# First mixer of a three-block kernel: the two gate products of a direction packed by row halves, with both bank waits of the second direction in front of its pair

## The chip, the cores and the metric

The kernel runs on one core of one Trainium2 chip. The metric is the device time of one execution in microseconds. Matrix products run on TensorE (PE in the profile), the other engines are ScalarE (ACT), VectorE (DVE), GpSimd (POOL) and SyncE (SP, which here only issues DMAs). Each has its own stream of instructions and waits on counting semaphores.

## The reference

One block of a gated recurrence with neighbourhood attention, then two layers of another kind, all on x of 512 tokens by 1024 channels in float32. What matters here is the recurrence of the first mixer:

```python
def _rglru_scan(xc, w_gates, b_gates, lam):
    xb = xc.reshape(B_, S, LRU_BLOCKS, LRU_BLOCK)          # 16 blocks of 64 channels
    gates = jnp.einsum('bsni,gnio->gbsno', xb, w_gates).reshape(2, B_, S, W)
    gates = gates + b_gates[:, None, None, :]
    r = jax.nn.sigmoid(gates[0])
    i = jax.nn.sigmoid(gates[1])
    log_a = -LRU_C * r * jax.nn.softplus(-lam)
    a = jnp.exp(log_a)
    bx = jnp.sqrt(-jnp.expm1(2.0 * log_a)) * (i * xc)
    _, h = lax.associative_scan(_lin_combine, (a, bx), axis=1)
    return h
```

It is computed twice, for the tokens forward and backward (two directions, each with its own weights). Each of the 16 blocks has its own 64x64 matrix for the gate r and for the gate i. Beside it stand a centred convolution that gives xc, attention over an 8x16 window with 16 heads of 64, and gating of both by projections.

## The kernel before

Channels lie on the 128 partitions and the 512 tokens along the free axis, so one tile of 128 channels holds two blocks of the recurrence and two heads. The large products (`unit(j)`) split each float32 operand into a high and a low fp32r part and take three products of 128x128 by 512 for each of 8 steps: 24 instructions at L1867 to L1869 for one unit. Before a unit can run, ACT rounds its raw weights to the high part wH (L1855) and DVE subtracts to get the low part wL (L1860).

The first mixer has eight bodies, p = 0 to 7, one for each tile of channels. Body p runs the seven units of the next tile (u = p + 1: xr, gr, q, k, v and two output gates) on PE, and between them the small products of its own tile; p = 1 to 6 are a hardware loop, and p = 7 has no units of its own but the first products of the output projection in their place. The order is written out by hand for each engine, and each `slot(j)` of ACT and DVE stands at the place of `unit(j)`. On PE a body is: unit(0), transposes of the previous tile's last probabilities (L522), **gates of direction 0**, the previous tile's second pair of P times V (L536), unit(1), statistics for q and k (L594), unit(2), **gates of direction 1**, four transposes of v (L601), unit(3), scores (L508), three more transposes of v (L608, after ACT has evacuated the first four), unit(4), and so on with probabilities, scores and P times V up to the next unit(0).

On ACT, after slot(3): Ln and Exp for the norms of q and k (L298, L301, each with a table load), `act_gates` of direction 0, slot(4), `act_gates` of direction 1, two square roots (L309, with a table load), the evacuation of v (L311), then q, slot(5), k, the rest of v (L320) and the exponentials of the probabilities (L235). The Ln stands behind the evacuation of gr (L219), which waits for the end of unit(1). DVE then scales the probabilities, runs the two scans (L383 to L388, with the split of slot(6) between them) and the remaining scores, ACT turns the last ones and begins slot(0) of the next body.

In `pe_gates` (L546) the weights of one gate and direction are a 128x128 matrix with the two 64x64 blocks on its diagonal and zeros elsewhere; each product is in plain float32, which the profile shows as two instructions. Gate r goes to bank 4 and gate i to bank 5, full 128 rows each, and ACT takes each bank with one tanh (sigmoid by tanh) of 128x512 (L249), adding the bias column of `hbg`. Direction 1 reuses the banks: its first product waits for the first tanh of direction 0, its second for the second. The scores after unit(3) use the same banks and wait for the tanh of direction 1. SP loads the gate weights of a tile (L180) after the gates of the previous one.

Of the kernel before, what the change touches and what calls it, by code (L numbers as in the profile page):

```python
# [14 lines left out]
P = 128  # L15
# [25 lines left out]
ACT = mybir.ActivationFunctionType  # L41
# [16 lines left out]
def wait(eng, sem, value):  # L58

    if not (isinstance(value, int) and value <= 0):  # L60
        eng.wait_ge(sem, value)
# [64 lines left out]
def gated_recurrence_mixer(k, st, t, site):  # L126
# [32 lines left out]
    run = scratch("m1", "run", [2, RUN])  # L159
    bias = scratch("m1", "bias", [2, 4, 256])  # L160
    mask = scratch("m1", "mask", [3, 256])
    gate_w = scratch("m1", "gate_w", [4, P])
    mx = scratch("m1", "mx", [8])
    den = scratch("m1", "den", [8])
    M = k.sems("m1_", "evac gab_free zeroed sqk g2 g2p gth gelu qk_stat qk_rs qk_rr qkn conv gates gate_act t2_sqrt lru ix "
# [72 lines left out]
    def act_probT(act, p, s):  # L238
        act.wait_ge(M.p_tr, 4 * p + (s + 1))
        wait(act, M.pv, 4 * p + (s - 1))  # L240
        act.activation(probT[:, s % 2], bank[6][:], ACT.Copy).then_inc(M.p_ev, 1)

    def act_gates(act, p, d):

        for g, dst in ((0, t2), (1, ti)):
            act.wait_ge(M.gates, 4 * p + (2 * d + g + 1))
            wait(act, M.lru, 6 * p + (3 * d - 3))
            n = (2 * d + g) * 8
            act.activation(dst[:, d], bank[4 + g][:], ACT.Tanh, scale=0.5, bias=k.colat(k.hbg, n, p))\  # L249
               .then_inc(M.gate_act, 1)  # L250
        act.wait_ge(M.gate_act, 8 * p + (4 * d + 1))
        act.wait_ge(M.qk_stat, 2 * p + 2)
        sc = k.colat(k.nsp4, 8 * d, p)
        act.activation(la[:, d], t2[:, d], ACT.Exp, scale=sc, bias=sc).then_inc(M.gate_act, 1)
        sc = k.colat(k.sp2, 8 * d, p)
        act.activation(t2[:, d], t2[:, d], ACT.Tanh, scale=sc, bias=sc).then_inc(M.gate_act, 1)

    def act(act, after):
        def body(p, units, prev, tail):
            u = p + 1  # L260

            def slot(j):
                if units and not (isinstance(u, int) and u == 0 and j < st.early):
                    k.split_hi(act, st, u, j)
                if not units and j < after.early:
                    k.split_hi(act, after, 0, j)
            slot(0)
            if tail:
                act_probT(act, p - 1, 2)
            if prev:  # L270
                evac(act, p, 5)
                for n in range(2):
                    wait(act, M.lru, 6 * p)
                    act.wait_ge(M.evac, PER * p + (3 + n))
                    act.activation(sqk[:, n], qk[:, n], ACT.Square).then_inc(M.sqk, 1)
                wait(act, M.y1, 2 * p)
                act.activation(g2[:], gr[:], ACT.Square).then_inc(M.g2, 1)
            slot(1)
            if tail:
                act_probT(act, p - 1, 3)  # L280
            if prev:
                evac(act, p, 6)
                act.wait_ge(M.g2p, 2 * p + 2)
                act.activation(g2[:], g2[:], ACT.Tanh, scale=GELU_C).then_inc(M.gth, 1)
            slot(2)
            if units:
                evac(act, u, 0)
            slot(3)
            if units:
                evac(act, u, 1)  # L290
            if tail:
                act.wait_ge(M.y_f, p)
                act.activation(k.tile_of(k.H, site.y + p - 1), y[:], ACT.Copy).then_inc(M.y_hi, 1)
            if prev:

                for n in range(2):
                    act.wait_ge(M.qk_stat, 2 * p + (n + 1))
                    act.activation(qkr[:, n], bank[6 + n][:], ACT.Ln, bias=k.eps_col[:]).then_inc(M.qk_rs, 1)  # L298
                for n in range(2):
                    act.wait_ge(M.qk_rs, 4 * p + (n + 1))  # L300
                    act.activation(qkr[:, n], qkr[:, n], ACT.Exp, scale=-0.5).then_inc(M.qk_rs, 1)  # L301
                act_gates(act, p, 0)
            slot(4)
            if prev:
                act_gates(act, p, 1)
                wait(act, M.hsum, p)
                for d in range(2):
                    act.wait_ge(M.gate_act, 8 * p + (4 * d + 4))
                    act.activation(sq[:, d], t2[:, d], ACT.Sqrt).then_inc(M.t2_sqrt, 1)  # L309
                act.wait_ge(M.v_tr, 2 * p + 1)  # L310
                act.activation(v_tok[:, 0:4], bank[6][:].rearrange("p (a n) -> p a n", a=4), ACT.Copy)\  # L311
                   .then_inc(M.v_ev, 1)
            if units:
                evac(act, u, 2)
            slot(5)
            if units:
                evac(act, u, 3)
            if prev:
                act.wait_ge(M.v_tr, 2 * p + 2)
                act.activation(v_tok[:, 4:7], bank[6][:, 0:384].rearrange("p (a n) -> p a n", a=3), ACT.Copy)\  # L320
                   .then_inc(M.v_ev, 1)
                act_probs(act, p, 0)
                act_probs(act, p, 1)
            slot(6)
            if units:
                evac(act, u, 4)
            if prev:
                act_probT(act, p, 0)
                act_probs(act, p, 2)
                act_probs(act, p, 3)  # L330
                act_probT(act, p, 1)
# [41 lines left out]
        dve.tensor_tensor(both, both, by, ALU.mult).then_inc(M.scaled, 1)  # L373

    def dve_ix(dve, p, d):
        dve.wait_ge(M.gate_act, 8 * p + (4 * d + 2))
        dve.scalar_tensor_tensor(ti[:, d], ti[:, d], 1.0, xc[:], ALU.add, ALU.mult).then_inc(M.ix, 1)

    def dve_lru(dve, p, d):
# [119 lines left out]
    def pe_score_pair(pe, p, pr):  # L499

        if pr == 0:
            pe.wait_ge(M.qkn, 2 * p + 2)
            pe.wait_ge(M.gate_act, 8 * p + 6)
        else:
            pe.wait_ge(M.biased, 8 * p + 4)
        for b in range(2):
            n = 2 * pr + b
            last = [pe.matmul(bank[4 + hh][:, 256 * b:256 * b + 256],  # L508
                              qkn[64 * hh:64 * hh + 64, 0, P * n:P * n + P],
                              qkn[64 * hh:64 * hh + 64, 1, KSTART[n] * ROWS:KSTART[n] * ROWS + 256],  # L510
                              start=True, stop=True) for hh in range(2)]
        for l in last:
            l.then_inc(M.scores, 1)
# [26 lines left out]
            l.then_inc(M.pv, 1)  # L540

    def pe_gates(pe, p, d):
        for g in range(2):
            if d == 1:
                pe.wait_ge(M.gate_act, 8 * p + (g + 1))
            pe.matmul(bank[4 + g][:], gate_w[:, 2 * d + g], xc[:], start=True, stop=True).then_inc(M.gates, 1)  # L546

    def v_ready(pe):
        return lambda f: pe.wait_ge(S.v_ready, site.v0 + f + 1)
# [2081 lines left out]
def laid_out(x):  # L2631
# [24 lines left out]
    out = shape_constants()  # L2656
    out["cols"] = np.ascontiguousarray(np.concatenate(pieces, 1))
    out["xT"] = np.ascontiguousarray(x["x"][0].T.reshape(DT, P, SEQ).swapaxes(0, 1))
    gates = np.zeros((8, P, 4, P), np.float32)
    g = x["lru_w_gates"][0].reshape(4, 8, 2, 64, 64)  # L2660
    for half in range(2):
        gates[:, 64 * half:64 * half + 64, :, 64 * half:64 * half + 64] = g[:, :, half].transpose(1, 2, 0, 3)
    out["gate_w"] = gates
    rpb = np.zeros((16, RPB_DR, RPB_W), np.float32)
    rpb[:, :, 16:16 + RPB_DC] = x["rel_pos_bias"][0]
# [38 lines left out]
```

## Time and profile before

| what | value |
|---|---|
| median of 3 runs | 2438.6 us (2436.75 to 2439.14) |
| the profiled execution: time, span | 2440.55 us, 2438.4 us |
| PE, DVE, ACT, POOL busy | 97%, 53%, 41%, 7% of the span |
| mean granted clock of PE | 0.986 |
| instructions at L546 | 64, 592 ns median |
| tanh at L249 | 32, some 675 ns each |
| the first mixer in the span | about 414 to 828 us |

The span is the time between the first and the last instruction in the trace, and the execution's time holds 2.15 us more around it. An instruction's duration on PE, ACT or DVE overlaps with that of the next one, so what it costs in a row of instructions is the distance between starts. "64*128 64x512" on a product means weights of 64 rows by 128 columns and a moving operand of 64 rows by 512 columns. In a timeline, brackets hold the idle time before the instruction and what ended it.

### The profile page before, as it was taken

The numbers are of one execution on the slowest core, as the hardware profiler recorded it, in microseconds if no ns is written. First come the engines' busy times: TensorE is split into PE (matmuls) and PEld (weight loads), VectorE is DVE, ScalarE is ACT, GpSimd is POOL, SyncE is SP. The second block draws the span as 40 slices with busy tenths as digits, with TensorE's granted clock in tenths as the row PEclk, the third lists the DMA queues.
The fourth block names the chain that finished last, engine by engine and source line by source line (L and its number), as shares of the span: only waits on it lengthen the run. The fifth ranks groups of instructions, "written<-read, shape, count | busy, mean of one in ns | idle before, by whom it ended". The sixth has DMA issues, their size and how long they took to land.

```text
span 2438.4 us, 30936 instructions
## 1 busy us (share of the span) xinstructions
PE 2360.7 (97%) x10918; PEld 1899.4 (78%) x10918; DVE 1299.3 (53%) x1832; ACT 994.9 (41%) x1481; POOL 176.7 (7%) x140
## 2 busy tenths in 40 slices
PE   8999999999999799999999989999989998999998
PEld 6888887777776588888877768888877766888887
DVE  5443436556666544443365566555248986655524
ACT  4223223676666532222234444333234454433322
POOL 0000002333554000000000000000000000000000
PEclk9999999999999899999999989999999999999999
DMA  4333322222223132233232222223313222232321
GB/s 162 97 100 102 102 90 84 86 88 97 89 73 99 38 101 95 95 111 104 70 102 83 86 69 84 97 96 109 100 47 104 70 70 69 78 103 95 117 95 47
DMA packets 62183, 219.91 MB, mean 90 GB/s; under 512 B 7664, under 2 KB 12272, under 8 KB 62112
## 3 DMA queue, kind: packets, MB, share of 16 engines
q1 hardware_dynamic: 60944, 216.86, 26.9%
q10 hardware_dynamic: 1168, 2.12, 0.3%
q8 instruction: 43, 0.70, 0.1%
q14 instruction: 28, 0.23, 0.0%
HBM read 216.83 MB, written 2.12 MB: 90 GB/s over the span
## 4 chain that ended last, share of the span: by engine, by line
PE 87%; ACT 5%; DVE 4%; issue 4%; ACTq 0%; DMA 0%; DVEq 0%; SPq 0%
PE bank L1867 27%; PE bank L1869 26%; PE bank L1868 26%; ACT m_prob L235 1%; PE bank L546 1%; DVE wL L1860 1%; ACT wH L1855 1%; PE bank L536 1%; PE bank L978 0%; PE bank L1006 0%; PE bank L988 0%; PE bank L1566 0%; PE bank L2239 0%; PE bank L2238 0%; PE bank L2237 0%
## 5 line engine op out<-in xcount | busy, mean ns | idle before, releaser
L1867 PE MATMUL bank<-H,wH 128*128 128x512 f32 x3012 | 1193.2, 396 | 34.9 <-DVE L L1941 15.4
L1869 PE MATMUL bank<-H,wL 128*128 128x512 f32 x3012 | 1176.9, 391 | 0.0
L1868 PE MATMUL bank<-L,wH 128*128 128x512 f32 x3012 | 1176.2, 390 | 0.0
L1860 DVE TENSOR_TENSOR wL<-raw,wH 128x1024 fp32r<-128x1024 f32 (+1 forms) x361 | 475.9, 1325 | 615.5 <-ACT wH L1855 615.5
L1867 PEld LDWEIGHTS bank<-H,wH 128*128 128x128 f32 x3012 | 567.9, 189 | 165.2 <-issue 22.4
L1869 PEld LDWEIGHTS bank<-H,wL 128*128 128x128 f32 x3012 | 567.8, 189 | 120.5
L1868 PEld LDWEIGHTS bank<-L,wH 128*128 128x128 f32 x3012 | 568.4, 189 | 118.7 <-issue 3.8
L1855 ACT ACTIVATE wH<-raw 128x1024 fp32r<-128x1024 f32 (+1 forms) x361 | 396.0, 1105 | 225.4 <-PE bank L1869 204.5
L2059 ACT ACTIVATE H<-prod 128x512 f32 (+1 forms) x88 | 55.7, 632 | 243.5 <-DVE prod L2124 243.5
L2104 DVE TENSOR_TENSOR gate_s<-bank,rstd 128x512 f32<-128x512 f32 x88 | 60.8, 691 | 113.7 <-PE bank L1869 110.7
L641 POOL TENSOR_TENSOR m_bias<-m_run,m_mask 128x256 f32<-128x256 f32 x64 | 75.8, 1221 | 408.1 <-DMA m_run<-in_rpb 408.1
L2124 DVE TENSOR_TENSOR prod<-silu_g,bank 128x512 f32<-128x512 f32 x88 | 60.3, 685 | 79.7 <-PE bank L1869 73.6
L1936 ACT ACTIVATE H<-xT,cols 128x512 fp32r<-128x512 f32 (+1 forms) x56 | 39.9, 723 | 149.5 <-DVE xT L2386 119.0
L2048 ACT ACTIVATE silu_g<-gate_s 128x512 f32<-128x512 f32 x44 | 27.9, 633 | 162.0 <-DVE gate_s L2104 162.0
L2051 ACT ACTIVATE silu_g<-gate_s,cols 128x512 f32<-128x512 f32 x44 | 35.9, 815 | 114.5 <-DVE gate_s L2104 114.5
L2115 DVE SCALAR_TENSOR_TENSOR silu_g<-gate_s,cols,silu_g 128x511 f32<-128x511 f32 x88 | 66.1, 751 | 30.7 <-ACT silu_g L2051 25.1
L2128 DVE TENSOR_TENSOR L<-prod,H 128x512 f32 (+1 forms) x88 | 60.1, 683 | 3.0 <-ACT H L2059 2.8
L2055 ACT ACTIVATE silu_g<-silu_g 128x512 f32<-128x512 f32 x44 | 27.8, 632 | 76.8 <-DVE silu_g L2115 76.8
L235 ACT ACTIVATE m_prob<-m_prob,m_mx 128x256 f32<-128x256 f32 x64 | 32.0, 501 | 66.3 <-DVE m_mx L363 66.2
L1374 DVE SCALAR_TENSOR_TENSOR m_acc<-m_gp,cols,m_acc 128x512 f32<-128x512 f32 x84 | 57.5, 745 | 0.0
L1916 ACT ACTIVATE square<-mixT 128x512 f32<-128x512 f32 (+1 forms) x28 | 17.7, 633 | 94.6 <-DVE mixT L2377 51.2
L1941 DVE SCALAR_TENSOR_TENSOR L<-xT,cols,H 128x512 fp32r<-128x512 f32 (+1 forms) x56 | 41.2, 745 | 4.6 <-ACT H L1936 4.6
(267 smaller groups left out, 1696.4 us busy)
## 6 DMA issues: line engine op xcount, KB each, us to landing
raw<-in_w_ffn_gu SPq DMA_DIRECT2D x88, 512.0 KB, 3.4
raw<-in_w_in SPq DMA_DIRECT2D x56, 512.0 KB, 3.9
raw<-in_w_ffn_down SPq DMA_DIRECT2D x32, 704.0 KB, 4.0
raw<-in_w_up_2a SPq DMA_DIRECT2D x44, 512.0 KB, 3.4
raw<-in_w_up_2b SPq DMA_DIRECT2D x44, 512.0 KB, 3.4
raw<-in_w_in_even SPq DMA_DIRECT2D x24, 512.0 KB, 4.4
raw<-in_w_in_odd SPq DMA_DIRECT2D x24, 512.0 KB, 3.4
raw<-in_w_down_2a SPq DMA_DIRECT2D x16, 704.0 KB, 4.3
```

The lines of the kernel that those rows point to most:

```text
L235: act.activation(prob[:, s % 2, 256 * b:256 * b + 256], prob[:, s % 2, 256 * b:256 * b + 256], ACT.Exp, bias=mx[:, e:e + 1], accum_out=den ...
L641: pool.tensor_tensor(bias[:, hh, n].rearrange("p (c r) -> p c r", r=ROWS), src, mask[:, MASK_OF[n]].rearrange("p (c r) -> p c r", r=ROWS), ...
L1374: dve.scalar_tensor_tensor(dst, src, w, dst, ALU.mult, ALU.add).then_inc(M.cv, 1)
L1855: act.activation(split_at(st, i, j)[0], raw_at(st, j), ACT.Copy).then_inc(S.hi_done, 1)
L1860: dve.tensor_tensor(w_l, raw_at(st, j), w_h.bitcast(F32), ALU.subtract).then_inc(S.lo_done, 1)
L1867: pe.matmul(out, w_h, xh[:, k0 + k], start=start and k == ks[0], stop=False)
L1868: pe.matmul(out, w_h, xl[:, k0 + k], start=False, stop=False)
L1869: last = pe.matmul(out, w_l, xh[:, k0 + k], start=False, stop=stop and k == ks[-1])
L2104: dve.tensor_tensor(gate_s[:, b], ffn_bank(i, 2 * b)[:], rstd[:], ALU.mult).then_inc(S.gate_ev, 1)
L2115: dve.scalar_tensor_tensor(silu_g[:, b, shift:], gate_s[:, b, 0:SEQ - shift], colr(w, (2 - shift) * FT + 2 * i + b), silu_g[:, b, shift:], ...
L2124: dve.tensor_tensor(prod[:, b], silu_g[:, b], ffn_bank(i, 2 * b + 1)[:], ALU.mult).then_inc(S.prod_done, 1)
L2128: dve.tensor_tensor(tile_of(L, ab + 2 * i + b), prod[:, b], tile_of(H, ab + 2 * i + b).bitcast(F32), ALU.subtract).then_inc(S.a_ready, 1)
```

## The change

The matrix of weights for a direction becomes two halves, one for each block of 64 input channels (rows 0 to 63 and rows 64 to 127). Each half has 64 rows and 128 columns: for the lower block the columns of r and then of i, for the upper block those of i and then of r. So a direction is two products on 64 rows in place of two on 128 rows, one on each row half of the array, into banks 4 and 5. Bank 4 then holds r of the lower block in rows 0 to 63 and its i in rows 64 to 127, bank 5 holds i of the upper block in rows 0 to 63 and its r in rows 64 to 127. ACT takes each bank with two tanh of 64x512, in all four per direction, two of which write to other rows than they read. Direction 1 now waits once, before its first product, for all four tanh of direction 0. The counter of gate activations goes up 12 in a body, not 8, and the waits on it (exp on ACT, square roots, ix on DVE, scores on PE) are changed to fit. The gate weights of a tile are half as large.

```diff
--- before.py
+++ after.py
@@ -159,7 +159,7 @@
     run = scratch("m1", "run", [2, RUN])
     bias = scratch("m1", "bias", [2, 4, 256])
     mask = scratch("m1", "mask", [3, 256])
-    gate_w = scratch("m1", "gate_w", [4, P])
+    gate_w = scratch("m1", "gate_w", [2, P])
     mx = scratch("m1", "mx", [8])
     den = scratch("m1", "den", [8])
     M = k.sems("m1_", "evac gab_free zeroed sqk g2 g2p gth gelu qk_stat qk_rs qk_rr qkn conv gates gate_act t2_sqrt lru ix "
@@ -240,15 +240,21 @@
         wait(act, M.pv, 4 * p + (s - 1))
         act.activation(probT[:, s % 2], bank[6][:], ACT.Copy).then_inc(M.p_ev, 1)
 
+    def rows_at(buf, rows, first, n):
+
+        return buf[rows, first + n:first + n + 1] if isinstance(n, int) else buf[rows, bass.ds(first + n, 1)]
+
     def act_gates(act, p, d):
 
-        for g, dst in ((0, t2), (1, ti)):
-            act.wait_ge(M.gates, 4 * p + (2 * d + g + 1))
-            wait(act, M.lru, 6 * p + (3 * d - 3))
-            n = (2 * d + g) * 8
-            act.activation(dst[:, d], bank[4 + g][:], ACT.Tanh, scale=0.5, bias=k.colat(k.hbg, n, p))\
-               .then_inc(M.gate_act, 1)
-        act.wait_ge(M.gate_act, 8 * p + (4 * d + 1))
+        lower, upper = slice(0, 64), slice(64, P)
+        wait(act, M.lru, 6 * p + (3 * d - 3))
+        for half, r_rows, i_rows in ((0, lower, upper), (1, upper, lower)):
+            act.wait_ge(M.gates, 4 * p + (2 * d + half + 1))
+            rows = (lower, upper)[half]
+            for g, dst, src in ((0, t2, r_rows), (1, ti, i_rows)):
+                act.activation(dst[rows, d], bank[4 + half][src, :], ACT.Tanh, scale=0.5,
+                               bias=rows_at(k.hbg, rows, (2 * d + g) * 8, p)).then_inc(M.gate_act, 1)
+        act.wait_ge(M.gate_act, 12 * p + (6 * d + 3))
         act.wait_ge(M.qk_stat, 2 * p + 2)
         sc = k.colat(k.nsp4, 8 * d, p)
         act.activation(la[:, d], t2[:, d], ACT.Exp, scale=sc, bias=sc).then_inc(M.gate_act, 1)
@@ -305,7 +311,7 @@
                 act_gates(act, p, 1)
                 wait(act, M.hsum, p)
                 for d in range(2):
-                    act.wait_ge(M.gate_act, 8 * p + (4 * d + 4))
+                    act.wait_ge(M.gate_act, 12 * p + (6 * d + 6))
                     act.activation(sq[:, d], t2[:, d], ACT.Sqrt).then_inc(M.t2_sqrt, 1)
                 act.wait_ge(M.v_tr, 2 * p + 1)
                 act.activation(v_tok[:, 0:4], bank[6][:].rearrange("p (a n) -> p a n", a=4), ACT.Copy)\
@@ -373,7 +379,7 @@
         dve.tensor_tensor(both, both, by, ALU.mult).then_inc(M.scaled, 1)
 
     def dve_ix(dve, p, d):
-        dve.wait_ge(M.gate_act, 8 * p + (4 * d + 2))
+        dve.wait_ge(M.gate_act, 12 * p + (6 * d + 4))
         dve.scalar_tensor_tensor(ti[:, d], ti[:, d], 1.0, xc[:], ALU.add, ALU.mult).then_inc(M.ix, 1)
 
     def dve_lru(dve, p, d):
@@ -500,7 +506,7 @@
 
         if pr == 0:
             pe.wait_ge(M.qkn, 2 * p + 2)
-            pe.wait_ge(M.gate_act, 8 * p + 6)
+            pe.wait_ge(M.gate_act, 12 * p + 10)
         else:
             pe.wait_ge(M.biased, 8 * p + 4)
         for b in range(2):
@@ -540,10 +546,10 @@
             l.then_inc(M.pv, 1)
 
     def pe_gates(pe, p, d):
-        for g in range(2):
-            if d == 1:
-                pe.wait_ge(M.gate_act, 8 * p + (g + 1))
-            pe.matmul(bank[4 + g][:], gate_w[:, 2 * d + g], xc[:], start=True, stop=True).then_inc(M.gates, 1)
+        if d == 1:
+            pe.wait_ge(M.gate_act, 12 * p + 4)
+        for half, rows in enumerate((slice(0, 64), slice(64, P))):
+            pe.matmul(bank[4 + half][:], gate_w[rows, d], xc[rows, :], start=True, stop=True).then_inc(M.gates, 1)
 
     def v_ready(pe):
         return lambda f: pe.wait_ge(S.v_ready, site.v0 + f + 1)
@@ -2656,10 +2662,12 @@
     out = shape_constants()
     out["cols"] = np.ascontiguousarray(np.concatenate(pieces, 1))
     out["xT"] = np.ascontiguousarray(x["x"][0].T.reshape(DT, P, SEQ).swapaxes(0, 1))
-    gates = np.zeros((8, P, 4, P), np.float32)
-    g = x["lru_w_gates"][0].reshape(4, 8, 2, 64, 64)
+    gates = np.zeros((8, P, 2, P), np.float32)
+    g = x["lru_w_gates"][0].reshape(2, 2, 8, 2, 64, 64)
     for half in range(2):
-        gates[:, 64 * half:64 * half + 64, :, 64 * half:64 * half + 64] = g[:, :, half].transpose(1, 2, 0, 3)
+        for gate in range(2):
+            at = 64 * (gate if half == 0 else 1 - gate)
+            gates[:, 64 * half:64 * half + 64, :, at:at + 64] = g[:, gate, :, half].transpose(1, 2, 0, 3)
     out["gate_w"] = gates
     rpb = np.zeros((16, RPB_DR, RPB_W), np.float32)
     rpb[:, :, 16:16 + RPB_DC] = x["rel_pos_bias"][0]
```

## Rows read from the trace of the kernel before

**Rows 1.** The page: engine shares, and the chain that ended last, by engine.

```profile
PE 2360.7 (97%) x10918; PEld 1899.4 (78%) x10918; DVE 1299.3 (53%) x1832; ACT 994.9 (41%) x1481; POOL 176.7 (7%) x140
...
PE 87%; ACT 5%; DVE 4%; issue 4%; ACTq 0%; DMA 0%; DVEq 0%; SPq 0%
```

**Rows 2.** Busy time by stretch, one body (p = 2): length, then each engine.

```profile
516.20:567.70 51.50, 51.16 (x251) 38.87 (x251) 32.54 (x53) 34.46 (x60) 22.30 (x18) 1.00 0.26 86
```

**Rows 3.** The chain in order of time, p = 2: start, length, what.

```profile
530.58 0.25 PE bank L1869
...
537.09 0.57 ACT m_t L249
...
545.62 0.48 ACT m_v_tok L311
...
552.66 0.70 DVE m_ti L383
...
566.25 1.43 DVE wL L1860
```

**Rows 4.** Timeline of PE, p = 2: start, length, idle before in brackets.

```profile
537.85 1.88 PE L546 MATMUL bank<-m_xc,m_gate_w 128*128 128x512 f32 x4
539.57 0.60 PE L601 MATMUL bank<-ident,m_vT 128*128 128x128 f32 x4
...
545.02 0.39 PE L1868 MATMUL bank<-L,wH 128*128 128x512 f32 x1
545.25 0.39 PE L1869 MATMUL bank<-H,wL 128*128 128x512 f32 x1
545.56 1.13 PE L508 MATMUL bank<-m_qkn 64*128 64x256 f32 x8
546.63 0.55 PE L608 MATMUL bank<-ident,m_vT 128*128 128x128 f32 x3
...
567.72 0.50 PE L1867 MATMUL bank<-H,wH 128*128 128x512 f32 x1 [0.35 <-DVE wL L1860]
```

**Rows 5.** Timeline of PE in the second mixer.

```profile
1284.43 1.13 PE L978 MATMUL bank<-m_qk 64*128 64x512 f32 x4
1285.49 0.55 PE L988 MATMUL bank<-ident,m_prob 128*128 128x128 f32 x3
```

**Rows 6.** Timeline of ACT, p = 2.

```profile
536.99 0.67 ACT L249 ACTIVATE m_t<-bank,hbg 128x512 f32<-128x512 f32 x1
537.56 0.68 ACT L249 ACTIVATE m_ti<-bank,hbg 128x512 f32<-128x512 f32 x1
538.13 0.81 ACT L254 ACTIVATE m_la<-m_t,nsp 128x512 f32<-128x512 f32 x1
...
545.52 0.58 ACT L311 ACTIVATE m_v_tok<-bank 128x512 f32<-128x512 f32 x1
```

**Rows 7.** Timeline, last body (p = 7), PE and ACT.

```profile
778.57 3.78 PE L546 MATMUL bank<-m_xc,m_gate_w 128*128 128x512 f32 x4 [3.71 <-DVE m_xc L438]
...
818.01 1.98 PE L536 MATMUL bank<-m_probT,m_v_tok 128*64 128x128 f32 x16 [10.05 <-issue]
...
789.85 0.69 ACT L298 ACTIVATE m_qkr<-bank,eps_col 128x512 f32<-128x512 f32 x1 [0.17 <-PE bank L594]
```

**Rows 8.** Groups of instructions, shapes kept apart, DVE: busy us, mean ns.

```profile
L958 DVE TENSOR_TENSOR m_table<-bank,m_dist_add 8x512 f32<-8x512 f32 x1 | 0.7, 672 | 0.0
```

**Rows 9.** Waits of SP's queue, p = 2: us in total, times, longest.

```profile
SPq L180 <- PE bank L546: 8.4, 1, 8.4
```

**Rows 10.** PE after two idles: timeline, and granted clock (before the DMA share).

```profile
413.81 0.47 PE L1867 MATMUL bank<-H,wH 128*128 128x512 f32 x1 [2.40 <-issue]
...
414.80:418.20 3.40, 3.40 (x10) 2.67 (x9) 3.33 (x3) 2.69 (x5) 3.23 (x4) 0.54 0.06 25
...
835.21 0.47 PE L1867 MATMUL bank<-H,wH 128*128 128x512 f32 x1 [1.64 <-DVE wL L1860]
...
834.00:838.00 4.00, 2.79 (x12) 2.34 (x13) 3.00 (x5) 2.19 (x3) 0.00 (x0) 1.00 0.40 129
```

## The prediction

> **What bounds the kernel now.** I read the page's engine shares and chain first [rows 1]. PE is busy 97% of the span and 87% of the chain that ended last, so a change that shortens PE work looks good. But the change sits in the first mixer, eight passes of one body, and its limit has to be read there. The busy time by stretch gives one body 51.5 us, with PE busy for all but 0.34 us of it and ACT for 34.5 us [rows 2]; the bodies of p = 1 to 6 agree within 0.1 us, one row standing for six.
>
> The timeline of PE says where those 0.34 us stand: one idle of 0.35 us before unit(0), ended by DVE's wL [567.72 in rows 4]; it stands so at the start of five bodies, p = 2 to 6. PE waits for data once per body, at its start. The chain of waits shows the loop behind it [rows 3]. From unit(0) through both halves of the early work to the end of unit(1) at 530.83 it is PE. Then ACT evacuates gr and is on the chain without a pause: y's high part, the tables and norms, the tanh of direction 0 at 537.09, v_tok at 545.62. From 552.66 it is DVE and ACT in turn up to the wL that ended at 567.68, and PE starts at 567.72 [rows 4]. So one turn of the loop is 14.5 us of PE, then 37 us of ACT and DVE beside which PE runs with only 0.35 us to spare. Both gate pairs are PE work, but d = 0 (before unit(1)) lies on the chain, and d = 1 (after unit(2)) lies beside it. The four tanh of both directions are ACT work on the chain.
>
> **The change part by part.**
>
> 1. *ACT: 2 tanh per direction become 4, of 64 rows each.* Two tanh of 128x512 start 0.57 us apart (536.99, 537.56), and the next operation starts 0.57 us after the second [rows 6]. No row shows a tanh on 64 rows. The nearest on the question of rows is DVE: an operation on 8x512 took 0.672 us [rows 8] and the same kind on 128x512 took 0.70 us [552.66 in rows 3]. It is the columns that cost. I take 0.57. A lower bound is the pitch of a plain copy out of a bank, 0.48 [v_tok, 545.62 in rows 3]. Per body there are 4 more instructions: 4 x 0.57 = 2.28 us, all of it inside the stretch that the chain gives to ACT without a pause. With 0.48 it is 8 x 0.48 - 4 x 0.57 = 1.56 us. Over 8 bodies: +18.2 (lower bound +12.5).
>
> The Trainium skill, "ScalarE: Activation LUTs", Rules for kernel authors, speaks against this change: it budgets about 0.3 us for each ACTIVATE with a bias pointer plus 0.83 ns an element. For 512 columns that is an estimate of 0.72 us, four more a body 2.9 us and eight bodies 23 us; rows 6 show 0.57 from start to start, and the measured pitch decides.
>
> 2. *PE, direction 0: the pair is packed by rows.* Today one direction is four instructions of 128 rows; from the first (537.85) to the next work (539.57) it is 1.72 us [rows 4]. The new form exists in the second mixer: four instructions of 64x512, two per row half, started at 1284.43 and the next work at 1285.49: 1.06 us [rows 5]. Entering the packed form costs a little more: the last product before the packed scores starts at 545.25 and the scores at 545.56, 0.31 us, where the product before it came 0.23 after its own (545.02, 545.25), so 0.08 to 0.09; I take 0.09. Saved: 1.72 - 1.06 - 0.09 = 0.57 us. Bounds: nothing if the halves don't overlap, 0.86 if they overlap without any cost (half of 1.72). On the chain in bodies 0 to 6: 7 x 0.57 = 4.0. What follows it there (the pair of P times V, unit(1), the statistics) has its inputs early, since no idle stands before any of them.
>
> The Trainium skill, "TensorE: Matmul & The Clock Gate", Part 3, gives packed tiles the time of one product plus 4 ns for each further tile. By that the pair would be about 0.86 us and the saving an estimate of 0.86 us a pair, 6.0 instead of 4.0; rows 5 show 1.06, and I use these.
>
> 3. *PE, direction 1: both waits in front of the pair.* Before, the first product needed only the first tanh (ended 537.66) and PE came at 537.85 [rows 4, 6]: nothing lost. Now the pair needs all four: 536.99 + 3 x 0.57 + 0.68 = 539.38, plus about 0.1. PE stands some 1.5 us; then the pair takes 1.06 (saving 0.57 of that). Net, what is queued behind it (v transposes, unit(3), scores) is 1.0 us later in reference to the end of unit(1). Who waits for it: ACT's direction 1 tanh, which come at 540.49 + 1.14 = 541.63, while the pair started at 539.5 is done by about 540.8. Not a stall. Next, PE's second v transposes (546.63) wait for ACT's v_tok, which ended at 545.52 + 0.58 = 546.10 [rows 6] and now ends at 548.38; PE comes at 547.6 and stands 0.8 us more. From unit(4) on PE is 1.8 us late, the chain 2.28, so the idle before unit(0) grows from 0.35 to about 0.8. Check: 1.5 + 0.8 + 0.8 = 3.1 us idle a body, and period + 1.71, work - 1.14, idle before 0.35 give 3.2. So this part costs nothing by itself: the cover is the ACT chain. Without that cover (if the tanh were cheap) it would cost the 1.0 us of PE lateness.
>
> 4. *Other queues.* SP waits on the gate counter before it loads the next gate weights, 8.4 us a body [rows 9], and now about 1 us longer; behind it in the queue are the table rows and the raw loads of the next body, whose first reader runs some 25 us later (wH before 566.25). The weights are half as large. DVE's ix waits for the fourth tanh, and unit(4) needs the split behind it only some 5 us later. POOL waits for the last scan and shifts with it. All at nothing; the DVE chain from 552.66 simply shifts.
>
> 5. *Last body.* PE stands idle 3.71 us and starts direction 0 at low clock, 3.78 us for four instructions [rows 7]. The packed pair at that clock is about 2.1, so 1.6 less, but a part is lost since the low clock then covers products instead. What it gives on the chain is small: ACT's second Ln waited for the second statistic until 789.85, and without waits could have started about 0.5 us sooner [rows 7]. I take -0.5. The stall of direction 1 is again under ACT's line, and after it PE waited 10 us for the chain of ACT and DVE anyway, so the 2.28 count in full.
>
> Sum: 18.2 - 4.0 - 0.5 = +13.7 us; body 0 has the same chain with under 0.1 us to spare: -0.1. **+13.6 us.** The profiled execution took 2440.55 us (span 2438.4 and 2.15 around it), which would become 2454.2; the median of the runs is 2438.6 and becomes **2452.2**. Ratio 0.9945, slower by 0.56%; about 0.2% (4.9 us) is what can be told from no change here.
>
> **Rivals.**
>
> *The halves don't overlap* (the scheduler of PE runs the four instructions one after the other). Against it: rows 5, where four instructions of 512 columns take 1.06 and not 1.72. Then direction 0 saves nothing: +18.2 - 0.1, 2456.7. 6%.
>
> *The granted clock falls in the new stalls.* In this trace an idle of 2.40 us at 413.81 was followed by a stretch of 3.4 us at a mean granted clock of 0.54, near the lower of its two levels, 1.2 GHz; in the 4 us around the idle of 1.64 us at 835.21 it was 1.00, the upper level, 2.4 GHz [rows 10]. The new idles are 1.5, 0.8 and 0.8, nearer the harmless one. A drop costs PE half of 3.4, 1.7 us, of which up to 0.5 is covered and by then the stall at v_tok (0.8) is filled: net up to 0.4 a body if it comes after the 1.5 stall, 1.7 if it comes at unit(0). Over 8 bodies that is 3 to 13 us above the forecast; with 6, 2458. 9%.
>
> *A 64-row tanh is cheaper than a 128-row one.* This would turn the sign. If it took half, 0.285, the ACT term is nothing and the saving stays: -4.6, 2434.0, within 0.2% just so; then the stall in front of direction 1 has less to cover too. The point from which it decides: 8 t = 4 x 0.57 + 0.57 gives t = 0.36 for no change. For it: no row shows ACT on fewer than 128 rows. Against it: the 8x512 row on DVE. 4%.
>
> *ACT's added time has a cover I don't see*, such as DVE waiting for something else at 552.66. Against it: the uniform 0.35 idle of five bodies, which is what a loop bound by another engine leaves. Then what is left is between -4.6 and 0, 2434 to 2438.6. 3%.
>
> **How the numbers follow.** The forecast has 78% (slower), no overlap 6% (slower), clock 9% (slower), cheap tanh 4% (3 same, 1 faster), cover 3% (same 2, faster 1). Its own bounds: low, tanh at 0.48 and half the way to the ideal pair: 12.5 - 5.0 - 0.5 = +7, 2445.6; high, no saving at all, +18.1, 2456.7, and some clock. The range leaves out the two cheap cases and the extremes: 2447.5 to 2457.5. Faster 0.02, same 0.05, slower 0.93.
>
> **What would show it.** In the profile after: 32 tanh more on ACT, 64x512, 0.57 apart (step 1); L546 then has 64 rows and from its start to the next work 1.06 (step 2); a PE idle near 1.5 before direction 1's pair, released by ACT, and one near 0.8 before the second v transposes (step 3); a period of a body 53.2 instead of 51.5, with PE idle near 0.8 before unit(0), released by wL as before. I am wrong if the tanh pitch is well below 0.57, if the period grows by other than 1.7, or if the granted clock in the bodies is below 1.00.

## The result and the profile after

The changed kernel takes 2461.6 us (2459.85 to 2462.8, 4 runs) against 2438.66: slower by 0.97%, ratio after over before 1.0097, 95% interval 1.0084 to 1.0109. The direction was forecast, the size was not: 22.9 us more where 13.6 stood, and above the end of the range, 2457.5.

The page of the profiled execution (2460.41 us, span 2458.6), the lines that answer to [rows 1]:

```profile
PE 2357.8 (96%) x10918; PEld 1895.9 (77%) x10918; DVE 1299.5 (53%) x1832; ACT 1019.7 (41%) x1513; POOL 177.6 (7%) x140
...
PE 84%; ACT 7%; DVE 4%; issue 4%; POOL 1%; ACTq 0%; DMA 0%; DVEq 0%; SPq 0%; POOLq 0%
```

PE is busy 2.9 us less, and its share of the chain has fallen from 87 to 84%. What it lost of the chain went to ACT (5 to 7%) and POOL (none to 1%).

The timeline of ACT in body p = 2, the lines that answer to [rows 6] (start, length, engine, line, what):

```profile
538.57 0.67 ACT L255 ACTIVATE m_t<-bank,hbg 64x512 f32<-64x512 f32 x1
539.26 0.69 ACT L255 ACTIVATE m_ti<-bank,hbg 64x512 f32<-64x512 f32 x1
539.97 0.68 ACT L255 ACTIVATE m_t<-bank,hbg 64x512 f32<-64x512 f32 x1
540.68 0.68 ACT L255 ACTIVATE m_ti<-bank,hbg 64x512 f32<-64x512 f32 x1
541.38 0.81 ACT L260 ACTIVATE m_la<-m_t,nsp 128x512 f32<-128x512 f32 x1
542.10 0.80 ACT L262 ACTIVATE m_t<-m_t,sp 128x512 f32<-128x512 f32 x1
542.81 1.04 ACT L1861 ACTIVATE wH<-raw 128x1024 fp32r<-128x1024 f32 x1
543.76 0.67 ACT L255 ACTIVATE m_t<-bank,hbg 64x512 f32<-64x512 f32 x1
```

Here the reader is to see two distances. A tanh on 64 rows lasts 0.67 to 0.69 us, as one on 128 rows did. But they start 0.69, 0.71, 0.71 us apart and la comes 0.70 after the last, where before a tanh started 0.57 after the last: the next instruction begins only when the one before has ended. From the first tanh to la it is 2.81 us and was 1.14. Exp, the in-place tanh and the rounding of wH behind them have kept their distances: 0.72, 0.71 and 0.95 (before 0.71, 0.70 and 0.95).

The timeline of PE in the same body, for [rows 4]:

```profile
518.45 0.50 PE L1873 MATMUL bank<-H,wH 128*128 128x512 f32 x1 [0.65 <-DVE wL L1866]
...
524.55 1.13 PE L552 MATMUL bank<-m_xc,m_gate_w 64*128 64x512 f32 x4
525.61 1.09 PE L542 MATMUL bank<-m_probT,m_v_tok 128*64 128x128 f32 x16
...
541.41 1.13 PE L552 MATMUL bank<-m_xc,m_gate_w 64*128 64x512 f32 x4 [1.82 <-ACT m_ti L255]
...
551.10 0.55 PE L614 MATMUL bank<-ident,m_vT 128*128 128x128 f32 x3 [1.44 <-ACT m_v_tok L317]
...
572.63 0.50 PE L1873 MATMUL bank<-H,wH 128*128 128x512 f32 x1 [0.64 <-DVE wL L1866]
```

In the kernel before, the body began with this line of PE's timeline and the next one with 567.72 in [rows 4]:

```profile
516.17 0.50 PE L1867 MATMUL bank<-H,wH 128*128 128x512 f32 x1 [0.35 <-DVE wL L1860]
```

The body is 54.18 us (518.45 to 572.63) and was 51.55. The packed pair takes 1.06 us to the next work, as the forecast had it from [rows 5]. The stalls are where they were expected. Two are longer: 1.82 us before the pair of direction 1 (about 1.5 expected) and 1.44 before the second transposes of v (0.8). The one before unit(0) is 0.64, a little less than the expected 0.8.

Two further places: the granted clock in a stretch of body p = 3 (the number before the DMA share), and PE at the end of the mixer:

```profile
597.10:600.50 3.40, 3.40 (x11) 2.77 (x10) 1.23 (x1) 3.33 (x5) 0.00 (x0) 0.54 0.31 81
...
836.37 1.97 PE L542 MATMUL bank<-m_probT,m_v_tok 128*64 128x128 f32 x16 [10.05 <-issue]
...
846.85 0.79 PE L1873 MATMUL bank<-H,wH 128*128 128x512 f32 x1 [1.35 <-DVE L L409]
...
855.41 0.47 PE L1873 MATMUL bank<-H,wH 128*128 128x512 f32 x1 [0.72 <-DVE wL L1866]
```

The line of the kernel before that answers to 846.85:

```profile
828.50 0.50 PE L1867 MATMUL bank<-H,wH 128*128 128x512 f32 x1 [1.35 <-DVE L L403]
```

After the 1.82 us idle the granted clock fell to 0.54, near its lower level, 1.2 GHz, in two of the six bodies that have this idle (p = 1 to 6). In the last body it fell behind an idle of 2.43 us (0.62 from 811.0 to 815.5). The lines at 846.85 and 855.41 show the hand-over to the output projection: from 846.85 to 855.41 it is 8.6 us, and was 6.7 (828.50 to 835.21, the latter in [rows 10]), since its first products ran at a granted clock of 0.50 (846.9 to 850.3) in this execution. Experiment 4, with the same work at this place, shows 1.00 there and 6.7 us, so this is not the change's in every execution. The wait of 10.05 us before 836.37 is the same as in [rows 7].

### The profile page after: what moved, and what is told of

It is laid out like the page before. It is cut to its first block, busy times and chain, and to the rows that moved or that the text cites. A ratio compares the mean times of both kernels' runs of the same rounds, so it can differ in the third digit from the quotient of the medians.

```text
span 2458.6 us, 30984 instructions
## 1 busy us (share of the span) xinstructions
PE 2357.8 (96%) x10918; PEld 1895.9 (77%) x10918; DVE 1299.5 (53%) x1832; ACT 1019.7 (41%) x1513; POOL 177.6 (7%) x140
## 4 chain that ended last, share of the span: by engine, by line
PE 84%; ACT 7%; DVE 4%; issue 4%; POOL 1%; ACTq 0%; DMA 0%; DVEq 0%; SPq 0%; POOLq 0%
PE bank L1873 26%; PE bank L1875 25%; PE bank L1874 25%; ACT m_ti L255 1%; ACT m_prob L235 1%; ACT m_t L255 1%; DVE wL L1866 1%; ACT wH L1861 1%; ACT m_la L260 1%; PE bank L984 0%; PE bank L1012 0%; PE bank L1572 0%; PE bank L994 0%; PE bank L2245 0%; PE bank L2244 0%
## 5 line engine op out<-in xcount | busy, mean ns | idle before, releaser
L1873 PEld LDWEIGHTS bank<-H,wH 128*128 128x128 f32 x3012 | 569.3, 189 | 167.0 <-issue 21.4
```

What stands on the lines that cost most here:

```text
L1873: pe.matmul(out, w_h, xh[:, k0 + k], start=start and k == ks[0], stop=False)
```

## The experiments

All ratios are against the kernel before, run on the same chip.

**1. The tanh alone is cut, PE stays.** Each tanh of 128x512 becomes two of 64x512 on their own rows; PE waits for two and for four of them.

```diff
         for g, dst in ((0, t2), (1, ti)):
             act.wait_ge(M.gates, 4 * p + (2 * d + g + 1))
-            act.activation(dst[:, d], bank[4 + g][:], ACT.Tanh, ...)
+            for rows in (slice(0, 64), slice(64, P)):
+                act.activation(dst[rows, d], bank[4 + g][rows, :], ACT.Tanh, ...)
...
```

> The kernel before with PE unchanged (four 128-row instructions per direction) and each tanh of 128x512 cut into two of 64x512, which read the rows that they write. The kernel after showed 0.69 to 0.71 us from start to start of its 64-row tanh, against 0.57 for the 128-row ones. Theory A (fewer than 128 rows is what costs): pitch 0.70, ACT + 3.3 us a body, about + 26 us. Theory B (reading other rows than are written costs): pitch 0.57, + 2.28 a body, about + 18 us. Theory C (two tanh in a row from the same bank cost): the first of each bank 0.57 after the one before, the second 0.70, together about + 22 us or more.

Measured: 2468.25 us, ratio 1.0125 (1.0104 to 1.0146). The timeline of ACT (two instructions to a line, x2):

```profile
541.60 1.38 ACT L253 ACTIVATE m_t<-bank,hbg 64x512 f32<-64x512 f32 x2
543.00 1.39 ACT L253 ACTIVATE m_ti<-bank,hbg 64x512 f32<-64x512 f32 x2
544.42 0.81 ACT L258 ACTIVATE m_la<-m_t,nsp 128x512 f32<-128x512 f32 x1
```

2.82 us from the first tanh to la, as in the kernel after. Theory B, that reading across rows costs, is out, since nothing is read across here. The split of ACT's work alone costs more than the whole change, 31 us. A body lasts 55.12 us (520.82 to 575.94) and 54.18 in the kernel after. Of the 0.94 between them the packing gives back some 0.7 (experiment 3), and 0.24 are two later starts on ACT, told at the end of the next section. Two bodies, p = 4 and 5, last 55.73 and 55.65: in them the granted clock fell to 0.51 and 0.50 behind the idle of 1.87 us in front of the second transposes of v (664.67 and 720.39), and no idle is left before their next unit(0).

**2. No crossing.** The kernel after with `src` replaced by `rows` in the tanh, so that each reads the rows that it writes. It leaves out the exchange between the halves, so half of the sigmoids come from the other gate's product.

```diff
-            for g, dst, src in ((0, t2, r_rows), (1, ti, i_rows)):
+            for g, dst, src in ((0, t2, rows), (1, ti, rows)):
```

> The kernel after, but each 64-row tanh reads the rows that it writes, so half of the sigmoids come from the other gate's product. Theory A: pitch 0.70 as in the kernel after, time the same within 1 us. Theory B: pitch 0.57, 8 x 0.13 = 1.0 us less a body, some 8 us less than the kernel after. Theory C: as A, since the banks follow each other as 4, 4, 5, 5.

Measured: 2461.1 us, 1.0092 (1.0072 to 1.0112), not to be told from the kernel after. But its timeline shows what none of the three theories said:

```profile
538.13 0.67 ACT L255 ACTIVATE m_t<-bank,hbg 64x512 f32<-64x512 f32 x1
538.70 0.67 ACT L255 ACTIVATE m_ti<-bank,hbg 64x512 f32<-64x512 f32 x1
539.39 0.68 ACT L255 ACTIVATE m_t<-bank,hbg 64x512 f32<-64x512 f32 x1
539.98 0.67 ACT L255 ACTIVATE m_ti<-bank,hbg 64x512 f32<-64x512 f32 x1
540.68 0.81 ACT L260 ACTIVATE m_la<-m_t,nsp 128x512 f32<-128x512 f32 x1
...
548.58 1.15 ACT L315 ACTIVATE m_sq<-m_t 128x512 f32<-128x512 f32 x2
549.75 0.60 ACT L317 ACTIVATE m_v_tok<-bank 128x512 f32<-128x512 f32 x1
```

The starts are 0.57, 0.69, 0.59 and 0.70 us apart. The second tanh of each pair has the short distance, though it has 64 rows and the bank of the one before; the long one stands where the rows change, lower to upper half and then to la. This gave theory D: the overlap with the instruction before is lost when the rows change. A body lasts 53.96 us, only 0.22 less than in the kernel after, though the tanh of both directions take 0.52 less together; the last line above is a part of the reason, and the end of the next section comes back to it.

**3. Packed pairs, whole tanh.** PE as in the kernel after, ACT as in the kernel before. It leaves out the sorting of r and i, which are mixed within a bank.

```diff
...
-            for g, dst, src in ((0, t2, r_rows), (1, ti, i_rows)):
-                act.activation(dst[rows, d], bank[4 + half][src, :], ACT.Tanh, ...)
+        for g, dst in ((0, t2), (1, ti)):
+            act.activation(dst[:, d], bank[4 + g][:], ACT.Tanh, ...)
...
```

> PE as in the kernel after (packed pairs, one wait for both banks), ACT as before: one tanh of 128x512 for each bank, so r and i are mixed within a bank. If ACT's added instructions are the whole loss, only the PE saving of direction 0 is left: 0.6 to 0.7 us a body, 5 us less than before, near 2433.5. If the packed form or its wait costs something that I have not seen, the time is at or above that of the kernel before.

Measured: 2433.64 us (10 runs), 0.9988 (0.9977 to 1.0). The interval reaches to no change, but the profile is plain (timeline of PE):

```profile
512.08 0.50 PE L1871 MATMUL bank<-H,wH 128*128 128x512 f32 x1 [0.50 <-DVE wL L1864]
...
533.50 1.13 PE L550 MATMUL bank<-m_xc,m_gate_w 64*128 64x512 f32 x4 [0.28 <-ACT m_ti L253]
...
562.91 0.50 PE L1871 MATMUL bank<-H,wH 128*128 128x512 f32 x1 [0.50 <-DVE wL L1864]
```

The body is 50.83 us, 0.72 less than before, and the clock stays at its upper level in the bodies p = 0 to 6. The packed form and its wait cost nothing here; the stall before direction 1's pair is 0.28 us and hidden. So the loss comes with the four tanh on ACT. That nothing more is lost by having both together is shown by the sum for the body in the next section.

**4. The banks alternate.** The kernel after, with both tanh of r first and then both of i, behind one wait for both products.

```diff
...
-            for g, dst, src in ((0, t2, r_rows), (1, ti, i_rows)):
+        act.wait_ge(M.gates, 4 * p + (2 * d + 2))
+        for g, dst, cross in ((0, t2, 0), (1, ti, 1)):
+            for half, rows in enumerate((lower, upper)):
+                src = (lower, upper)[half ^ cross]
...
```

> The kernel after with another order of the four tanh: both of r (banks 4, 5), then both of i (banks 4, 5), with the wait for both products in front. r is read on its own rows, i crosses. Theory A: pitch 0.70 throughout, time as the kernel after. Theory B: 0.57 for r, 0.70 for i, some 4 us less. Theory C: 0.57 throughout, some 8 us less than the kernel after.

Measured: 2460.12 us, 1.0094 (1.0072 to 1.0116). The timeline of ACT:

```profile
538.30 1.38 ACT L255 ACTIVATE m_t<-bank,hbg 64x512 f32<-64x512 f32 x2
539.70 1.39 ACT L255 ACTIVATE m_ti<-bank,hbg 64x512 f32<-64x512 f32 x2
541.12 0.81 ACT L260 ACTIVATE m_la<-m_t,nsp 128x512 f32<-128x512 f32 x1
```

2.82 us to la: no change by the order of the banks, theory C is out. Theory A, that 64 rows cost, would say the same; it is the timeline of experiment 2 that speaks against it.

**5. Split, ordered by rows.** The first kernel of this series with both tanh of rows 0 to 63 first (the edit is shown against that kernel). On PE the first product of direction 1 now waits for three tanh.

```diff
+        act.wait_ge(M.gates, 4 * p + (2 * d + 2))
-        for g, dst in ((0, t2), (1, ti)):
-            act.wait_ge(M.gates, 4 * p + (2 * d + g + 1))
-            for rows in (slice(0, 64), slice(64, P)):
+        for rows in (slice(0, 64), slice(64, P)):
+            for g, dst in ((0, t2), (1, ti)):
...
```

> The first split kernel (PE unchanged, four 64-row tanh a direction, all on their own rows) with another order: both of rows 0 to 63, then both of rows 64 to 127, behind one wait for both products. Theory D, formed from the first four runs: a tanh starts 0.57 us after the one before it where both read and write the same rows, and 0.70, the whole duration of the one before, where the rows that are read or written change. Then the pitches are 0.57, 0.70, 0.58, 0.70, together 2.55 where the first split kernel has 2.81: 0.5 us less a body, 4 us less in all. Theory A (any tanh of 64 rows costs 0.70): no difference from it.

Measured: 2462.49 us, 1.0104 (1.0087 to 1.0121); the body is 54.61 us where the first split kernel has 55.12. The timeline of ACT:

```profile
540.42 0.67 ACT L253 ACTIVATE m_t<-bank,hbg 64x512 f32<-64x512 f32 x1
540.99 0.67 ACT L253 ACTIVATE m_ti<-bank,hbg 64x512 f32<-64x512 f32 x1
541.68 0.68 ACT L253 ACTIVATE m_t<-bank,hbg 64x512 f32<-64x512 f32 x1
542.27 0.67 ACT L253 ACTIVATE m_ti<-bank,hbg 64x512 f32<-64x512 f32 x1
542.97 0.82 ACT L258 ACTIVATE m_la<-m_t,nsp 128x512 f32<-128x512 f32 x1
```

0.57, 0.69, 0.59, 0.70, 2.55 us in all: as theory D said, and theory A said no difference.

**6. Rows 64 to 127 first.** The same kernel with the two halves in reverse order, one run.

```diff
-        for rows in (slice(0, 64), slice(64, P)):
+        for rows in (slice(64, P), slice(0, 64)):
```

> The kernel with unchanged PE and the four tanh ordered by rows, with rows 64 to 127 first. Theory D says 'a change of rows' costs the overlap of about 0.12 us; it leaves open whether that is a change of the number of rows or of the first row. If it is the first row: the piece before the first tanh is lengthened (Exp to tanh 0.64 where it was 0.53), then 0.57, 0.70, 0.58, and the last tanh (rows 0 to 63) is followed by la, on 128 rows, after 0.57. If it is the number of rows: la comes 0.70 after it as before.

Measured: 2462.54 us, one run (2438.82 for the kernel before beside it). The timeline of ACT:

```profile
540.27 1.15 ACT L305 ACTIVATE m_qkr<-m_qkr 128x512 f32<-128x512 f32 x2
541.45 0.68 ACT L253 ACTIVATE m_t<-bank,hbg 64x512 f32<-64x512 f32 x1
542.03 0.67 ACT L253 ACTIVATE m_ti<-bank,hbg 64x512 f32<-64x512 f32 x1
542.73 0.68 ACT L253 ACTIVATE m_t<-bank,hbg 64x512 f32<-64x512 f32 x1
543.31 0.67 ACT L253 ACTIVATE m_ti<-bank,hbg 64x512 f32<-64x512 f32 x1
543.88 0.81 ACT L258 ACTIVATE m_la<-m_t,nsp 128x512 f32<-128x512 f32 x1
```

It is the first row, not their number: la on 128 rows follows the tanh on rows 0 to 63 after 0.57 us, and the second Exp (128 rows, started at 540.27 + 0.53 = 540.80) is now followed by the tanh on rows 64 to 127 only after 0.64 to 0.65, where the whole tanh and the lower half came 0.52 after it.

**7. One wait for each product.** The kernel after with the wait in front of the pair undone.

```diff
-        if d == 1:
-            pe.wait_ge(M.gate_act, 12 * p + 4)
         for half, rows in enumerate((slice(0, 64), slice(64, P))):
+            if d == 1:
+                pe.wait_ge(M.gate_act, 12 * p + (2 * half + 2))
```

> The kernel after with one wait for each product of direction 1: the lower half waits for two tanh, the upper for all four. If the chain of ACT decides, PE's earlier start is hidden and the time is that of the kernel after within 1 us, with the body at 54.2 us; the upper half starts at the same moment as before, so even PE's next work comes no sooner. If the wait in front of the pair is itself what costs, up to 1.4 us a body come back, 11 us.

Measured: 2460.28 us, 1.009 (1.0071 to 1.011). The timeline of PE:

```profile
520.59 0.50 PE L1873 MATMUL bank<-H,wH 128*128 128x512 f32 x1 [0.64 <-DVE wL L1866]
...
542.14 1.12 PE L552 MATMUL bank<-m_xc,m_gate_w 64*128 64x512 f32 x2 [0.41 <-ACT m_ti L255]
543.56 1.12 PE L552 MATMUL bank<-m_xc,m_gate_w 64*128 64x512 f32 x2 [0.29 <-ACT m_ti L255]
...
574.78 0.50 PE L1873 MATMUL bank<-H,wH 128*128 128x512 f32 x1 [0.64 <-DVE wL L1866]
```

The lower half now starts 1.42 us before the upper one, which waits for the fourth tanh as ever; the body is 54.19 us. Putting both waits in front cost nothing.

**8. and 9. ACT is relieved of 0.48 us.** The first evacuation of v goes from ACT to DVE, once in the kernel after and once in the kernel before.

```diff
-                act.wait_ge(M.v_tr, 2 * p + 1)
-                act.activation(v_tok[:, 0:4], bank[6][:].rearrange(...), ACT.Copy).then_inc(M.v_ev, 1)
...
                 dve_ix(dve, p, 1)
+                dve.wait_ge(M.v_tr, 2 * p + 1)
+                dve.tensor_copy(v_tok[:, 0:4], bank[6][:].rearrange(...)).then_inc(M.v_ev, 1)
```

> The kernel after with the first evacuation of v (128x512 out of bank 6) taken from ACT and given to DVE, which stands idle 5 us just there. If ACT's stretch is what sets the body's period, its 0.48 us come off each body: 53.7 instead of 54.2, 4 us less than the kernel after. If PE set it, nothing changes but PE's 1.44 us stall before the second transposes of v goes.

> The kernel before with the same evacuation on DVE. ACT's chain shortens by 0.48 us a body, but PE has only 0.35 us idle a body to give: the period falls from 51.55 to 51.2, 2.5 to 3 us in all, and the idle before unit(0) goes. Near the bound of what can be told.

Measured: 2454.33 us, 1.0076 (1.0056 to 1.0095), and 2436.36 us (10 runs), 0.9992 (0.9982 to 1.0002). The timelines of PE, first the kernel after with the move, unit(0) of two bodies:

```profile
517.10 0.50 PE L1872 MATMUL bank<-H,wH 128*128 128x512 f32 x1 [0.28 <-DVE wL L1865]
...
570.83 0.50 PE L1872 MATMUL bank<-H,wH 128*128 128x512 f32 x1 [0.25 <-DVE wL L1865]
```

then the kernel before with it, the gates of direction 0 of two bodies:

```profile
518.20 1.88 PE L545 MATMUL bank<-m_xc,m_gate_w 128*128 128x512 f32 x4
...
569.22 1.88 PE L545 MATMUL bank<-m_xc,m_gate_w 128*128 128x512 f32 x4
```

The bodies are 53.73 us (0.45 less than 54.18) and 51.02 (0.53 less than 51.55, where 0.35 was expected). Taking 0.48 us from ACT shortens the body by nearly as much in the kernel after: its period is ACT's. The whole time is 6 us less than that of experiment 7, its neighbour on the same chip, where 4 were expected; 1.7 of the 6 is the hand-over, at a higher clock in the trace of this one (6.72 us against 8.44).

In the kernel before with the move, the idle before unit(0) is gone and PE sets the period. The timelines of PE differ in a body at one place only: from the last transposes (L522, L521 here) to unit(0) it was 1.01 us and is 0.50. So PE had 0.5 us to give and not 0.35: the bracket counts from the end of the transposes, and where nothing is waited for, unit(0) starts 0.16 before that end. This kernel is quicker than the kernel before in its body, but its time can't be told from it.

**10. The kernel before once more.** One run, for a second trace.

> The kernel before, unchanged, for a second trace of it. In its first trace PE's idle of 2.40 us at 413.81 was followed by 3.4 us at a clock of 0.5, and the traces of seven other kernels of this study, equal up to that point, mostly show 1.6 us there and no drop. If that differs from execution to execution, this trace shows the first gate product near 417.5 instead of 421, the same body of 51.55 us, and a span some 3 us shorter.

Measured: 2439.98 us, span 2437.5. The timeline of PE:

```profile
413.11 0.47 PE L1867 MATMUL bank<-H,wH 128*128 128x512 f32 x1 [1.68 <-issue]
...
418.65 1.88 PE L546 MATMUL bank<-m_xc,m_gate_w 128*128 128x512 f32 x4
...
815.12 1.98 PE L536 MATMUL bank<-m_probT,m_v_tok 128*64 128x128 f32 x16 [10.06 <-issue]
```

The idle is 1.68 us and the first gates stand at 418.65, not 420.97: the head of the mixer differs between executions of one kernel by 2.3 us. The span is only 0.9 us shorter: from 2015 to 2023 us the granted clock was 0.57 in this execution and 1.00 in the first. From the first gates to the P times V pair after the long idle it is 396.5 us here, 397.0 in the first trace.

## Why the prediction was wrong in size

**The step that failed** is the first term, "I take 0.57". The row on DVE said that columns cost and not rows, and for the length of a tanh that held: 0.68 us on 64 rows as on 128. But the term needed the distance between starts, and in these traces that is 0.11 us shorter than the length only while the first row read and the first row written stay the same. In the kernel after it changes at each of the four tanh and again at la. Per direction 2.81 - 1.14 = 1.67 us, per body 3.34 instead of 2.28, over 8 bodies 26.7 instead of 18.2: 8.5 us more. I had a bound from below (0.48) and none from above. One from above stood in [rows 6]: with no overlap at all the distance is about the length, 0.68, and 8 x (8 x 0.68 - 4 x 0.57) = 25.3 would have put the high end at 2464. Even this was passed by a little, since the measured distances are 0.02 to 0.03 above the length.

**The packed pair** came out as said: 1.06 us to the next work. In front of P times V the old pair had taken 1.81 and not 1.72, so the saving on the chain is 1.81 - 1.06 less 0.08 for the entry = 0.67 instead of 0.57; over 7 bodies 0.7 us more in the change's favour. The whole-tanh experiment shows it by itself: 0.72 a body. 3.34 - 0.67 = 2.67, and the body grew by 2.63, where the prediction had 1.71 and named any other growth as a sign of being wrong.

**The chain of ACT and the cover of direction 1** held. The stalls of 1.82 and 1.44 us lie beside ACT's work: undoing the wait changed nothing, taking 0.48 from ACT gave 0.45. They are longer than 1.5 and 0.8 by ACT's longer tanh. One reading was off without harm to the sum: what PE had to spare in the kernel before was 0.5 us a body and not the 0.35 of the bracket (experiment 9).

**The last body** I had as 2.28 less 0.5; from its first gates to the pair after the long idle it is 42.14 us (794.23 to 836.37) against 39.44, so 2.7. Of ACT's 3.34 that leaves 0.64 for all that was saved there, near the 0.5.

**The granted clock** fell in two of the bodies p = 1 to 6, as the rival had it, but without its price: the bodies with a drop (487.9 and 597.1 in the trace) last 54.25 and 54.22, the others 54.18 to 54.20. It was not luck of this trace: in experiment 4 three bodies have such a drop and last 54.20 to 54.22, and in experiment 8 three with one last 53.73 and two without 53.76 and 53.77. PE had idle time left behind the drop, before the transposes of v or before unit(0), and it took that up. Where a drop stood later and had less idle behind it, it cost: 0.5 to 0.6 us in two bodies of experiment 1. At the hand-over it cost 1.85 us (8.56 for 6.71) in this trace, and about as much in those of experiments 2 and 7 (8.56 and 8.44), but not in those of 4 and 8 (6.69 and 6.72). So it differs from execution to execution.

**The sum again:** from the first gates to the pair after the long idle 418.6 us (417.73 to 836.37) against 397.0, + 21.6; by the terms, 26.7 for ACT less 4.7 for seven pairs and 0.6 in the last body is 21.4. With 1.85 at the hand-over it is 23.5, and the medians differ by 22.9. The span of the profiled executions differs by only 20.2, since the first trace of before lost about 3 us at the head of the mixer (gates at 420.97 against 417.73) that no other trace lost in full (gates at 417.4 to 419.9 in them).

That ACT loses its overlap where the first row changes is shown by the pattern in the timelines of all these kernels; what in the engine does it was not tried. One confusion is left: the bias of a tanh is a column on the rows that are written, so where the rows written change, those of the bias change too, and no run tells the two apart. That a change of the rows read is enough by itself is shown (second tanh of the kernel after, 0.69).

**The row of the last read of a bank.** Two starts come late without a change of rows from one instruction to the next. In experiments 1, 2 and 5 the first tanh of direction 1, on rows 0 to 63, comes 1.06 to 1.07 us after wH on 128 rows, and v_tok comes 0.63 to 0.64 after the second square root (the last two lines of experiment 2: 549.75 - 548.58 = 1.17, of which the first square root takes 0.54); in the kernels that cross, in experiment 3 and in the kernel before it is 0.95 and 0.52. Both late ones read a bank, and all that lies between them and the tanh before reads no bank. In experiments 1, 2 and 5 the last tanh read its bank from row 64, in all others from row 0. In experiment 6, which ends on row 0, v_tok comes after 0.52 again, and it is the tanh of direction 1, now from row 64, that comes after 1.07 or 1.08. So the rows fit this: an instruction that reads a bank keeps the overlap only where it begins on the row on which the last read of a bank began, even when others that read no bank stand between. It holds in every body p = 0 to 6 of the twelve traces; experiment 2 differs from the kernel after in the rows read alone and shows both late starts. No run was made to test it. The two late starts, 0.12 + 0.12 us, also close sums that the tanh alone leave open: experiment 1, 2 x (2.82 - 1.14) + 0.24 = 3.60, and the body grew by 3.57; experiment 5, 2 x (2.55 - 1.14) + 0.24 = 3.06, and it grew by 3.06.

The Trainium skill, "Perfetto Trace Analysis", Optimizing Scalar/DVE Operations, says that the profiled length holds an acknowledgement that overlaps with the next instruction. The 0.57 for a length of 0.68 agrees with it; that the overlap goes when the first row changes is measured here and not stated there. The Trainium skill, "ScalarE: Activation LUTs", Rules for kernel authors, gives by its figures an estimate of 0.72 us for such an ACTIVATE; that is near the 0.70 of the split tanh and far from the 0.57 of the whole ones. The prediction had set it aside for the measured 0.57, which [rows 6] showed for one shape and one set of rows only.

## What to carry to other kernels

Cost the consumer of a packed product with the producer: two row halves that hold different things need twice the instructions to read them, and where the reader's engine sets the period, that costs more than the packed product gives. Where a known instruction is to be used in a new shape or on other rows, put its whole length, and a little more, as the upper bound of its distance from start to start. And when instructions on row halves can't be avoided, order them so that those with the same first row follow each other (0.5 us of 5.6 a body here, less what a later read of a bank loses where it starts on another row than the last one did: 0.2 in experiment 2).

## What the runs showed of the hardware

- ACT: a tanh of 512 columns lasts 0.67 to 0.69 us on 64 and on 128 rows. The next instruction starts 0.57 to 0.59 us after it when the first row stays the same, and 0.69 to 0.71 us when the first row of what is read or of what is written, and of the bias with it, changes. In the kernel after, a change of the rows read alone gave 0.69 and 0.71, one of the rows written with the bias 0.71. The number of rows made no difference: 64 to 128 on the same first row gave 0.57, 128 to 64 gave 0.52 behind an Exp, as 128 to 128 did.
- ACT, a pattern not tested by a run of its own: an instruction on row 0 that reads a bank came 0.12 us late when the last earlier read of a bank began at row 64, though three or four instructions that read no bank stood between.
- The granted clock of PE was 0.54 in a stretch of 3.4 us behind the idle of 1.82 us in two bodies of the kernel after, and stayed at 1.00 behind the same idle in four others; neither changed the body's length by more than 0.07 us. In experiment 1 a clock of 0.50 to 0.51 behind an idle of 1.87 us later in the body made it 0.5 to 0.6 us longer.
- The idle that a bracket shows on PE can be less than what a wait costs: 0.35 us in the bracket before unit(0), 0.51 us from start to start.
